# Sample tile first: a new order of TensorE, ScalarE and VectorE ahead of the expert gathers of a one-core decoder step

## What is computed

```
def token_mixer(xn, ...):
    q, k, v, gu, gv = split(xn @ w_in)              # 1024 -> 512, 128, 128, 512, 512
    attn = sliding-window attention(rope(q), rope(k), v, sinks)
    sgu  = gelu(gu) * (w_s @ rms_norm(gelu(gv)) + b_s)      # the "gating"
    return concat[rms_norm(attn), rms_norm(sgu)] @ w_out

def memory_attention(xn, mem_k, mem_v, w_cq, w_co): ...

def peer_ffn(xn, ...):                    # per token: 8 heads x 16 experts
    q = xn @ w_pq
    s1, i1 = top_k(q_first_half  @ sub_keys, 16)
    s2, i2 = top_k(q_second_half @ sub_keys, 16)
    top, sel = top_k(all 256 sums, 16); idx = expert numbers
    h = einsum('td,thkd->thk', x, u_tab[idx])
    return einsum('thk,thkd->td', gelu(h) * softmax(top), v_tab[idx])
```

## Time and profile before

| | |
|---|---|
| runs | 1710.36 us median of 3 (1703.64 to 1710.81) |
| profiled execution | 1710.95 us, of which the span of instructions is 1709.2 us |
| busy | PE 76%, DVE 68%, ACT 47%, POOL 37% of the span |
| mean granted TensorE clock | 0.868 of full |
| moved by DMA | 657.35 MB, mean 385 GB/s; 604.28 MB of it on the gathers' queue |
| first gather issued | at 198.57 us |

### The profile page before, as it was taken

One profiled execution on the slowest core, in us unless ns is written; L12 is line 12 of the kernel. 1 busy time (PEld: TensorE's weight loads), 2 busy tenths in 40 slices (PEclk: granted clock), 3 DMA queues, 4 the chain that ended last, 5 costly groups with the idle time before them and its releaser, 6 DMA issues.

```text
span 1709.2 us, 21622 instructions
## 1 busy us (share of the span) xinstructions
PE 1297.9 (76%) x7069; PEld 474.0 (28%) x7069; DVE 1165.4 (68%) x2796; ACT 809.6 (47%) x2338; POOL 636.4 (37%) x584
## 2 busy tenths in 40 slices
PE   9999977887888776677877776777777667667665
PEld 4455522433434322123322111111111111111110
DVE  2544567887667677777777777767666677677764
ACT  1434355775444355455555454455444445444443
POOL 0000043443434344444444444443444444444441
PEclk9999888899999887889898777888888987888866
DMA  9433699999999999999999999999999999999995
GB/s 357 164 142 129 260 370 421 406 371 419 421 420 421 420 394 403 422 394 422 421 421 419 421 421 421 421 422 421 420 421 422 420 416 421 422 421 416 422 415 223
DMA packets 99041, 657.35 MB, mean 385 GB/s; under 512 B 12576, under 2 KB 17568, under 8 KB 22368
## 3 DMA queue, kind: packets, MB, share of 16 engines
q0 software_dynamic: 83056, 604.28, 85.7%
q1 hardware_dynamic: 15872, 51.68, 8.0%
HBM read 652.71 MB, written 4.19 MB: 384 GB/s over the span
## 4 chain that ended last, share of the span: by engine, by line
DMA 46%; PE 25%; DVE 12%; ACT 10%; issue 7%; POOL 1%; ACTq 0%; DVEq 0%; SPq 0%; POOLq 0%
DMA R<-in_peer_uv,R 45%; PE ps L2028 9%; PE ps L1562 6%; DVE R L1481 4%; PE ps L1821 2%; ACT L918 2%; ACT R L927 2%; ACT R L922 1%; PE ps L1534 1%; ACT R L918 1%; DVE R L1295 1%; DVE R L1296 1%; DVE R L1298 1%; ACT L833 1%; PE ps L1546 1%
## 5 line engine op out<-in xcount | busy, mean ns | idle before, releaser
L2028 PE MATMUL ps<-R 64*64 64x512 f32 x4528 | 730.2, 725 | 375.8 <-ACT R L927 375.6
L647 POOL DMA_INDIRECT R<-in_peer_uv,R x566 | 623.1, 1101 | 964.5 <-PE ps L2028 774.6
L1481 DVE CUSTOM_DVE_ANT_0 R<-R 128x1024 f32<-128x1024 f32 x566 | 687.9, 1225 | 383.0 <-DMA R<-in_peer_uv,R 376.3
L918 ACT ACTIVATE R<-R 128x1 f32<-128x1 f32 x576 | 115.9, 201 | 611.9 <-DVE R L1481 610.9
L2028 PEld LDWEIGHTS ps<-R 64*64 64x64 f32 x4528 | 134.0, 149 | 723.8 <-ACT R L927 648.7
L927 ACT ACTIVATE R<-R 128x64 f32<-128x64 f32 x576 | 200.3, 348 | 54.9 <-ACT R L922 1.9
L1821 PE MATMUL ps<-A,R 128*128 128x256 f32 (+1 forms) x640 | 222.2, 474 | 0.0
L922 ACT ACTIVATE R<-R 128x1 f32<-128x1 f32 x576 | 169.7, 295 | 20.9
L1821 PEld LDWEIGHTS ps<-A,R 128*128 128x128 f32 (+1 forms) x640 | 95.3, 199 | 258.0 <-issue 256.9
L1562 PE MATMUL ps<-A,R 128*128 128x512 f32 (+1 forms) x256 | 101.1, 547 | 0.0
L918 ACT ACT_TABLE_LOAD x60 | 77.0, 1283 | 7.1 <-DVE R L1481 6.1
(11 more groups left out here) (300 smaller groups left out, 941.3 us busy)
## 6 DMA issues: line engine op xcount, KB each, us to landing
R<-in_peer_uv,R POOLq DMA_INDIRECT x566, 16.0
A<-in_w_pq SPq DMA_DIRECT2D x8, 1024.0 KB, 10.2
A<-in_w_in SPq DMA_DIRECT2D x3, 2048.0 KB, 20.1
R<-in_w_out SPq DMA_DIRECT2D x5, 1024.0 KB, 9.2
x_res<-in_x_prompt SPq DMA_DIRECT2D x6, 512.0 KB, 9.3
R<-in_w_out SPq DMA_DIRECT2D x1, 3072.0 KB, 9.8
R<-in_x_promptT SPq DMA_DIRECT2D x4, 512.0 KB, 7.6
R<-in_w_cq SPq DMA_DIRECT2D x2, 1024.0 KB, 10.8
```

What stands on the lines that cost most here:

```text
L647: pool.indirect_dma_start(slots[slot_of[g]], None, I["peer_uv"][:, :], bass.IndirectOffsetOnAxis(ap=idx[:, b % 4, k:k + 1], axis=0)).then_ ...
L918: act.activation(hgelu[:, b % 2, col], hdot[:, b % 2, col], ACT.Gelu).then_inc(gelu_ready, 1)
L1481: dve.tensor_tensor_reduce(u, u, xn(t), 1.0, 0.0, ALU.mult, ALU.add, hdot[:, b % 2, k:k + 1]).then_inc(u_used, 1)
L2028: ins = pe.matmul(bank(2 * (t % 2) + q)[rows], diag[tokens, g % DIAGS, :], v_rows[slot_of[g]][tokens, c * 512:(c + 1) * 512], start=first, ...
```

## The change

Five things change, and nothing of the arithmetic.

1. **TensorE's order.** Everything that only tiles 3 and 4 need is moved back: project(3, 2) (but its first eighth), project(4, 2), gating(3), gating(4), heads_T(3), heads_T(4), half_T(3), half_T(4) go behind scores(0), some into the expert loop at fixed g through a new function `beside(g)`. So do the transposes and the values product of tile 1, attn_T(1) and both halves of `out_one` (in one piece each, at g = 2 and g = 4, with project(4, 2) between them at g = 3).
2. **ScalarE's and VectorE's order** follows: gates_out(3) and (4), qkT_evac(3) and (4), half_norm(3) and (4) on ScalarE and gated, half_rows and half_take of tiles 3 and 4, top_keys(1, .), attn_scaled(1), attn_take(1) and add_one on VectorE move into the loop; half_norm(2), values_out, queries_out(4), keys_out(4) move within the head. With them, some results land in other PSUM banks.
3. **Slots.** The first four gathers have slots 9 and 8 alone. Slots 1 and 2 join at g = 4, 3 and 4 at g = 8 (where slot 8 leaves), 5 at 14, 0 at 18. Slot 8 can be used early, as it is free from the sample tile's memory attention and the first sub keys.
4. **Loads.** The sub keys of the heads of the first two queries are loaded ahead as four DMAs of 128 KB into a place of their own (`sk_early`); all of skT is loaded later, behind `h_tr` 3. The pieces of w_pq are laid out in another order and wait for other signals: piece 5 behind `l_pv`, piece 1 behind `pkv_done` 5, piece 3 behind `n_tr` 1, pieces 2 and 6 behind `pgu_done` 5, piece 7 behind `mixed_done` 5.
5. **Due times** of tile 1 and partly tile 2 (`PREP_AT` and so on) are 3 later; the queries of block 2 start at g = 9 instead of 0, those of block 12 at 170 instead of 167.

The diff, cut to its core:

```diff
-SLOT_PHASES = ((0, (0, 9, 1, 2, 3, 4)), (14, (0, 9, 1, 2, 3, 4, 5)), (31, (0, 1, 2, 3, 4, 5, 7, 9)),
-               (74, ...
+SLOT_PHASES = ((0, (9, 8)), (4, (1, 2, 9, 8)), (8, (3, 4, 1, 2, 9)), (14, (3, 4, 1, 2, 9, 5)),
+               (18, (0, 9, 1, 2, 3, 4, 5)), (34, (0, 1, 2, 3, 4, 5, 7, 9)), (77, ...
-        PREP_AT = {1: 1, 2: 122, 3: 200, 4: 210}
+        PREP_AT = {1: 4, 2: 125, 3: 200, 4: 210}
-        LATE = {4: 8, 12: 7}
-        QUICK = (12,)
+        LATE = {2: 9, 4: 8, 12: 10}
+        QUICK = (2, 12)
...
@@ SP queue
-            sp.wait_ge(h_tr, 2)
+            sp.wait_ge(h_tr, 1)
+            sp.wait_ge(qkT_done, 3)
             load(w_co, ...)
...
             sp.wait_ge(l_sc, 1)
             for h in (0, 4):
                 load_wpq(h)
-            sp.wait_ge(h_tr, 3)
+            sp.wait_ge(l_pT, 1)
+            for n, h in enumerate((0, 4, 1, 5)):
+                load(sk_early[:, n], I["sub_keysT"][:, h * 256:(h + 1) * 256], ld_sk)
+            sp.wait_ge(l_pv, 1)
+            load_wpq(5)
+            sp.wait_ge(h_tr, 2)
             load(g_ffn, ...)
-            load(skT, I["sub_keysT"][:, :], ld_sk)
...
@@ POOL
                     elif slot_of[g] == 8:
-                        pool.wait_ge(l_add, 2 * (TILES - 1))
+                        pool.wait_ge(l_oT, 1)
+                        pool.wait_ge(pq_s, 2)
...
@@ TensorE, head
-            project(3, 2)
             sample_rows()
             gating(1, bank(6))
-            project(4, 0)
+            project(3, 3, 0, 2)
             sample_T(xn(0), p_tr, True)
-            gating(2, bank(6))
+            project(3, 3, 2, 4)
             halves_beside(...)              # wo_done 1
-            half_T(1)
-            project(3, 3, 0, 5)
+            project(4, 0, 0, 4)
             sample_T(xn(0), p_tr, False)
-            project(3, 3, 5, KD)
-            heads_T(3)
-            half_T(2)
+            project(4, 0, 4, 5)
             (query product, w_cq)
...
+            project(4, 0, 6, KD)
+            project(3, 3, 4, KD)
+            half_T(1)
+            project(4, 3)
             (memory scores)
...
+            q_T(0)
+            scores(0)
+            (transposes of tile 1's probabilities)
+            q_mm(1)
+            (values of tile 1)
+            q_T(1)
+            project(3, 2, 1, 4)
+            scores(1)
+            project(3, 2, 4, KD)
+            gating(3, bank(6))
+
+            def beside(g):
+
+                if g == 0:
+                    attn_T(1, o_one, bank(3))
+                elif g == 2:
+                    out_one(0)
+                elif g == 3:
+                    project(4, 2)
+                elif g == 4:
+                    out_one(1)
+                elif g == 5:
+                    heads_T(3)
+                elif g == 7:
+                    half_T(3)
+                    gating(4, bank(6))
+                elif g == 9:
+                    heads_T(4)
+                elif g == 11:
+                    half_T(4)
+                elif g == 13:
+                    pe.wait_ge(h_T, 4)
+                    pe.wait_ge(ld_sk, 80)
```

More of the change, by code:

```diff
@@ L213, in hybrid_step @@
         w_co = v3(R[:, 12288:14336], 2)
-        skT = R[:, 14336:16384]
-        g_ffn = R[:, 16384:17408]
+        g_ffn = R[:, 14336:15360]
+        skT = R[:, 15360:17408]
         triu = R[:, 17408:17536]
@@ L789, in _ @@
             act.activation(pT_c, v3(bank(5), 4), ACT.Copy).then_inc(l_pTo, 1)
-            values_out(4)
-            half_norm(3)
+            half_norm(2)
             gating_std(4)
+            act.wait_ge(l_oT, 1)
+            act.activation(oT_c, v3(bank(5)[:, 0:P], 2), ACT.Copy).then_inc(l_oTo, 1)
+            act.wait_ge(x2_out, 1)
+            act.wait_ge(p_tr, 2)
+            row_norm(0, xn(0), f_std, ss_f)
+            count(act.activation(stat[:, 126:127], eps[:, 0:1], ACT.Exp))
+            act.wait_ge(f_tr, 1)
+            act.activation(T0, v3(bank(7), KD), ACT.Copy).then_inc(f_out, 1)
             act.wait_ge(sc_max, 2)
@@ L1740, in _ @@
             ins.then_inc(qs_T, 1)
-            project(4, 3, 1, 3)
-            pe.wait_ge(qkT_out, 8)
-            gating(3, bank(6))
+            project(4, 0, 6, KD)
+            project(3, 3, 4, KD)
+            half_T(1)
+            project(4, 3)
             pe.wait_ge(qbd_out, 1)
@@ L1750, in _ @@
             ins.then_inc(l_sc, 1)
-            project(4, 3, 3, KD)
+            gating(2, bank(6))
             pe.wait_ge(l_exp, 1)
@@ L1774, in _ @@
             ins.then_inc(l_pv, 1)
-            project(4, 2, 4, 6)
+            half_T(2)
             pe.wait_ge(l_o, 1)
@@ L1786, in _ @@
                 .then_inc(l_wo, 1)
-            half_T(3)
-            pe.wait_ge(sgu_out, 4)
-            heads_T(4)
-            pe.wait_ge(sc_exp, 2)
-            pe.wait_ge(gu_out, TILES)
-            pe.wait_ge(gv_out, TILES)
-            for h in range(HEADS):
-                ins = pe.transpose(ps[:, 1024 + h * P:1024 + (h + 1) * P], s_one[:, h, :], ident[:, :])
-            ins.then_inc(pT_done, 1)
-            pe.wait_ge(qkT_out, 10)
-            gating(4, bank(6))
+            pe.wait_ge(h_T, 2)
+            project(4, 1, 0, 6)
             pe.wait_ge(xn_low, 1)
             sample_T(xn(0), f_tr, False)
-            pe.wait_ge(pT_out, 3)
-            for h in range(HEADS):
-                ins = pe.matmul(bank(0)[:, h * HD:(h + 1) * HD], pT_one[:, h, :],
-                                v_rows_of(1)[:, (h // 4) * HD:(h // 4 + 1) * HD], start=True, stop=True)
-            ins.then_inc(pv_done, 1)
+            project(4, 1, 6, KD)
             def heads_of(s):
@@ L1841, in scores @@
                     for c in range(2):
-                        ins = pe.matmul(bank(5)[r, 256 + c * P:256 + (c + 1) * P], qT_sb[:, c, r],
-                                        skT[:, (2 * h + c) * P:(2 * h + c + 1) * P], start=True, stop=True)
+                        keys = early_heads(s)[:, 2 * j + c] if s < 2 else skT[:, (2 * h + c) * P:(2 * h + c + 1) * P]
+                        ins = pe.matmul(bank(5)[r, 256 + c * P:256 + (c + 1) * P], qT_sb[:, c, r], keys, start=True,
+                                        stop=True)
                 ins.then_inc(pq_s, 1)
@@ L1863, in _ @@
-            pe.wait_ge(h_T, 4)
-            def out_one(c, first, end):
-                for k in range(first, end):
-                    ins = pe.matmul(bank(2 + c), T1[:, k, :], w_out[:, 2 * c:2 * c + 2, k, :], start=(k == 0),
-                                    stop=(k == KD - 1))
-                if end == KD:
-                    ins.then_inc(wo_done, 1)
-            out_one(0, 0, 2)
-            q_T(1)
-            out_one(0, 2, 4)
-            scores(1)
-            out_one(0, 4, KD)
-            out_one(1, 0, KD)
+            pe.wait_ge(pT_out, 3)
@@ new lines, in _, with out_one @@
+            for h in range(HEADS):
+                ins = pe.matmul(bank(0)[:, h * HD:(h + 1) * HD], pT_one[:, h, :],
+                                v_rows_of(1)[:, (h // 4) * HD:(h // 4 + 1) * HD], start=True, stop=True)
+            ins.then_inc(pv_done, 1)
+            q_T(1)
[3 more added lines that the diff above has]
+            gating(3, bank(6))
+            def out_one(c):
+                pe.wait_ge(n_T, 1)
+                pe.wait_ge(h_T, 1)
+                for k in range(KD):
+                    ins = pe.matmul(bank((3, 7)[c]), T1[:, k, :], w_out[:, 2 * c:2 * c + 2, k, :], start=(k == 0),
+                                    stop=(k == KD - 1))
+                ins.then_inc(wo_done, 1)
```

235 lines of the change are left out of this document (133 added, 102 removed).

## The result

The changed kernel takes 1728.69 us (median of 4 runs, 1724.24 to 1732.29), the kernel before 1710.59 beside it: ratio 1.0113, 95% interval 1.0091 to 1.0136. The profiled execution took 1725.81 us, its span is 1724.0 us. Forecast were 1703.4 us and a range up to 1716. The change makes the kernel 1.1% slower, and neither the forecast nor a rival had the place where it does so.

What follows compares the result with a forecast made beforehand. Full DMA engines bound the body, so only its start could move. Of gather 0's 24 us, 5.5 to 8.5 would last, taken as 7: 1710.95 - 7 = 1704.0, from the median 1703.4 us; range 1692 to 1716.

Steps and rivals of the forecast that it cites:

- Steps (a) to (h): Head, sample tile's chain from its output product to gather 0: gather 0 goes at about 174.5, 24 us earlier.
- the two values I had: Head, length of q_mm(0): 6.04 us at TensorE's lower clock, 3.66 if not; 6.04 was taken.
- R3: Gathers 2 to 4: TensorE's lower clock slows three long products by 21 us in all, time 1724; chance 0.10.
- R4: Whole run: all 24 us of gather 0's lead are kept, time 1686; chance 0.04.
- 14 gathers and all loads are through near 237: Start of the loop: this byte count was put near 237 us, against 245.5 in the kernel before, 8.5 earlier.
- the 7 us that are kept: Lead left at the start of the body, taken between 5.5 and 8.5 us.
- if the new one does so too: DMA rate at 224 to 248 us: a repeat of 362 GB/s instead of 420 leaves 5.5 us of lead.
- a turn of 9, so nothing: Between gathers 14 and 18, six slots for seven: 15 us of transfer per 9 us slot turn, no cost.
- R2: Head: gather 8 comes 7 us later than forecast, the lead is 0 and the time 1710.4; chance 0.20.
- The later due times of tile 1 leave one gather before q_mm(4) starts: Expert loop: tile 1's later due times still leave one gather before q_mm(4), listed under what costs nothing.
- from 300 us on the same GB/s: Body after 300 us: the profile should show the same DMA rate as the kernel before.
- if the body is slower by itself: Body: one of the conditions under which the prediction called itself wrong, beside gather 8 above 222 or below 209.

Runs made afterwards that it cites:

- the clean pair: Old head against new head at equal due times and attn_take, slots and block 2's start differing too: 1.0049 old, 1.0039 new, each against the kernel before.
- the first: Kernel before with only the later due times (3 gathers) and the slot phases that go with them: 1731.9 us, ratio 1.0151.
- twelfth experiment: Second measurement of the kernel before with only the due times 3 later and their slot phases: 1732.46 us, ratio 1.0133.
- e15: Kernel before, own slots, with tile 1's four due times 3 later and units at 27, 33, 39, 45, 51, 57: 1733.67 us, ratio 1.0135.
- e13: Changed kernel with units at 27, 33, 39, 45, 51, 57, out_piece, tile 2 and block 12 as before, slot phase at 73: 1724.53 us, 1.0092.

## Why the prediction was wrong

**Right.** The bound: body full of DMA, the lead counted in bytes. Steps (a) to (h): output product at 112.73 (said 113.7), w_cq 125.46 (126.6), memory scores 141.94 (143.0), memory values 151.51 behind their DMA (151), w_co 157.54 (155.4), q_mm(0) 166.85 (164.3), gather 0 at 175.56 (174.5). q_mm(0) took 4.14, between the two values I had. Part of the nearness of gather 0 is luck: q_mm(0) started 2.6 us late, and the way from it to gather 0 took 8.7 us instead of 10.2. Over all traces of the new head gather 0 went 18 to 24 us earlier. Gather 4 at 200.78 (199 to 202), gather 8 at 216.95 (215). R3 was rightly held small: the products took 7.13 us, with a granted clock of 1.00 from 180 to 220 us, that is 2.4 GHz. The Trainium skill's rule that activity releases the throttled clock (TensorE: Matmul & The Clock Gate, Part 1) held without harm here: the trace agrees with it, as the idle times ahead of these products were under 2 us and the clock stayed up. R4 was wrong as said.

**Wrong in size: "14 gathers and all loads are through near 237", the 7 us that are kept.** Gather 8 was 2 us late, skT and the last piece of w_pq were issued at 229.96 and 231.65, not near 223, and the rate behind it was 299 and then 346 GB/s, not 420: the 6.8 MB that the changed kernel still has to move at 224 us (50.1 MB there, 56.9 at the mark) take 20 us, until 244. That leaves under 2 us, the 1.7 of the windows. I had allowed 3 us for the rate "if the new one does so too", and for six slots "a turn of 9, so nothing". In their place stand the chain of 7 us behind out_one(1), which holds the next gather's gelu (TensorE waits 5.11 us; ScalarE's spare 11 of 24 us, an average, was no cover for it), and slot 5's tenant, whose products come at 235 and 239 and hold gather 14 for 6.73. So R2 was nearest here, with 0.20, and it named the wrong place (gather 8, where I said 7 us; it was 2).
What the new head is worth over the whole run was read three times: 0.10% in the clean pair, 0.26% between the first and twelfth experiment and the two measurements of the changed kernel, where the waits for w_out (11.3 and 11.8 against 5.1 and 5.3 us) make the difference (some 6 us between gathers 80 and 100), and 0.43% between e15 and e13, whose slot phases differ (a wait of 9.02 against 6.39 us for slot 7 is part of it). How much of the last two is the head's own isn't settled; at the due times that serve both heads best it is 1 to 2 us, and the intervals hardly leave room for 7.

**Wrong in sign: "The later due times of tile 1 leave one gather before q_mm(4) starts", and "from 300 us on the same GB/s".** Under the heading of what costs nothing I weighed the queries of blocks 2 and 12 and q_mm(4), and left out the units, attn_take, add_acc, out_piece and w_out. The due times, with the slot phases, cost 24 us with the old head (1.0142 on average), against the 7 us forecast as gain. The kernel before held the warning: the wait of 4.97 us at 388.21, where TensorE asked two gathers too early at little or no cost (without it the ratio is 0.9988, 0.9973 to 1.0004). Such a wait is where a shift by three gathers becomes dear, since other steps are tied to the ends of blocks and don't shift. For w_out the question would have been what goes right ahead of it in the queue: with slot 9's last gather at 73 instead of 67, the rows of x do. But that wait, at 5 us, cost nothing that could be measured; at 11 us, with the last gather at 75, it cost some 6. That no rival of mine lay behind 300 us is the real failure; R3 was the only slower one, and the range ended at 1716 for want of another. What stands in the place of "same GB/s from 300 us on": 6.2 MB less moved by 700 us, or 15 us; the early asks for attn_take account for 7 us and tile 2's later work for 4, and the later units and preparation of tile 1 cost 6 and 5 us with the old head.

**Step by step of what the profile should show:** products of 7.1 us, yes; DMA share low between 165 and 190, yes (0.40); low again near 215, no (1.00 from 212 to 218); 1.0 from 218, no (0.91 until 248); gather 8 within 209 and 222, yes; same GB/s from 300 us, no, and "if the body is slower by itself" was the condition that came true.

## What to carry to other kernels

In a software-pipelined loop with hand-set due times, a step's place is relative to those on the other engines and to the ends of blocks. Before shifting a group of due times, list for each wait who asks at which iteration, who answers at which, and what else the answering engine does in between; an ask one to three iterations ahead of its answer made the asking engine wait 1.8 to 10.3 us here. One that costs nothing today may cost after the shift: 4.97 us could be taken out without a measurable gain, 7.23 us (with one of 3.82) was worth 7. For a load, look at its landing too, and at what was queued right ahead of it. A lead at the start is worth only what is left of it in bytes once all slots turn: follow it gather by gather through the first twenty, with each slot's earlier tenant, before giving it a value.

## What was not expected of the hardware

Nothing in the durations: long products, dot products and table loads took what the rows of before say. New to me was how far profiled executions of one order differ in the head: gather 0 of the new head was issued between 174.91 and 180.68 us in twelve traces, and between 175.56 and 178.62 in the two traces of the changed kernel, while the medians of that kernel agree within 0.13%. A lag of 3 us at the end of one trace decides nothing, and the verdicts here rest on the ratios.
